# Forget-gate sums of the first attention: from selector matmuls to a DMA broadcast into the bias tile, with three weight tiles ahead of the head loop

## The reference

```python
z = h @ w_in                                   # (256 tokens, all projections)
fq, fk, fv, ff, dq, dk, dv, ga, gb = split(z)  # ff: 8 columns, the forget gates
log_f = log_sigmoid(ff + b_fgate)              # (8 heads, 256)
F = cumsum(log_f, axis=-1)                     # along the tokens
s = einsum('hqd,hkd->hqk', q, k) * scale + F[:, :, None] - F[:, None, :]
p = softmax(where(k_pos <= q_pos, s, -inf))    # 8 "fox" heads of width 64
o_a = einsum('hqk,hkd->hqd', p, v)
# then 4 "diff" heads (two softmaxes each), gates, output projections,
# a mixture of 32 experts, and a second block with attention and convolution
```

## Time and profile before

| what | value |
| --- | --- |
| median of three runs | 1005.55 us |
| the profiled execution, own time | 1005.98 us |
| its span | 1004.2 us |
| busy: PE, DVE, ACT, POOL | 909.9 (91%), 362.0 (36%), 321.0 (32%), 116.9 (12%) us |
| DMA over the span | 308.62 MB, mean 307 GB/s |
| shares of the chain that ended last | PE 67%, DMA 20%, DVE 4%, issue 3% |

### The profile page before, as it was taken

One profiled execution on the slowest core, in us unless ns is written; L12 is line 12 of the kernel. 1 busy time (PEld: TensorE's weight loads), 2 busy tenths in 40 slices (PEclk: granted clock), 3 DMA queues, 4 the chain that ended last, 5 costly groups with the idle time before them and its releaser, 6 DMA issues.

```text
span 1004.2 us, 26158 instructions
## 1 busy us (share of the span) xinstructions
PE 909.9 (91%) x12047; PEld 788.9 (79%) x12047; DVE 362.0 (36%) x740; ACT 321.0 (32%) x554; POOL 116.9 (12%) x78
## 2 busy tenths in 40 slices
PE   7999999999989898987878777779999999999997
PEld 7887789977767676765656556569989999999995
DVE  4356356843111111111111111125334344873475
ACT  5546646631000000000000000125346555554443
POOL 2110021000000000000000000003311112341122
PEclk9999999999999998999899988899999999999998
DMA  8995296899999999999999999999554444455101
GB/s 283 382 348 187 95 347 231 344 426 404 403 426 424 425 424 425 424 424 426 425 425 426 426 426 424 424 357 369 200 213 168 164 175 169 169 184 202 57 1 43
DMA packets 70861, 308.62 MB, mean 307 GB/s; under 512 B 5152, under 2 KB 11728, under 8 KB 58584
## 3 DMA queue, kind: packets, MB, share of 16 engines
q1 hardware_dynamic: 66816, 302.08, 75.7%
q10 hardware_dynamic: 3928, 4.80, 1.4%
HBM read 305.81 MB, written 2.63 MB: 307 GB/s over the span
## 4 chain that ended last, share of the span: by engine, by line
PE 67%; DMA 20%; DVE 4%; issue 3%; ACT 2%; SPq 2%; POOL 1%; another core or an unknown queue 1%; POOLq 0%; DVEq 0%; ACTq 0%
PE bank L789 66%; DMA ring<-in_w 10%; DMA arena<-in_w 10%; SPq L854 2%; DVE arena L1352 1%; DVE wR L1346 1%; DMA ring<-in_w_in 1%; PE bank L1011 1%; DVE arena L1349 1%; POOL wR L2272 1%; DVE arena L1346 0%; ACT wR L1918 0%; DVE hTR L1352 0%; DVE hTR L1346 0%
## 5 line engine op out<-in xcount | busy, mean ns | idle before, releaser
L789 PE MATMUL bank<-hTR,wR 128*128 128x256 f32 x2520 | 314.3, 285 | 4.3 <-DVE hTR L1352 1.6
L789 PE MATMUL bank<-arena 128*32 128x128 f32 (+7 forms) x4378 | 277.9, 324 | 43.2 <-DMA arena<-in_w 27.3
L789 PEld LDWEIGHTS bank<-hTR,wR 128*128 128x128 f32 x2520 | 305.4, 192 | 8.3 <-issue 4.2
L789 PEld LDWEIGHTS bank<-arena 128*32 128x32 f32 (+5 forms) x4378 | 211.2, 142 | 97.7 <-issue 66.6
L1346 DVE TENSOR_TENSOR wR<-ring,wR 128x1024 fp32r<-128x1024 f32 x108 | 136.9, 1274 | 118.0 <-ACT wR L1918 117.7
L1918 ACT ACTIVATE wR<-ring 128x1024 fp32r<-128x1024 f32 x137 | 143.3, 1054 | 91.0 <-PE bank L789 88.3
L789 PE MATMUL bank<-ring,arena 128*32 128x128 f32 (+3 forms) x2352 | 103.7, 319 | 30.9 <-DMA ring<-in_w 22.0
L789 PEld LDWEIGHTS bank<-ring,arena 128*32 128x32 f32 (+1 forms) x2352 | 68.9, 114 | 51.0 <-issue 31.5
L2063 ACT ACTIVATE arena<-bank,small 128x256 f32<-128x256 f32 x32 | 15.1, 473 | 272.2 <-PE bank L789 272.2
L2272 POOL TENSOR_TENSOR wR<-ring,wR 128x1024 fp32r<-128x1024 f32 x29 | 70.7, 2437 | 265.9 <-ACT wR L1918 265.9
L1680 DVE COPY arena<-bank 128x256 f32<-128x256 f32 x32 | 13.6, 425 | 193.4 <-PE bank L789 193.4
(11 more groups left out here) (190 smaller groups left out, 669.3 us busy)
## 6 DMA issues: line engine op xcount, KB each, us to landing
arena<-in_w SPq DMA_DIRECT2D x53, 2048.0 KB, 39.6
ring<-in_w SPq DMA_DIRECT2D x42, 2048.0 KB, 40.1
ring<-in_w_in SPq DMA_DIRECT2D x25, 2048.0 KB, 10.3
ring<-in_w_ada SPq DMA_DIRECT2D x5, 2048.0 KB, 11.2
arena<-in_w_in SPq DMA_DIRECT2D x4, 2048.0 KB, 13.1
ring<-in_w_o_attn SPq DMA_DIRECT2D x2, 2048.0 KB, 8.3
ring<-in_w_out SPq DMA_DIRECT2D x2, 2048.0 KB, 7.9
ring<-in_w_in SPq DMA_DIRECT2D x2, 1024.0 KB, 9.0
```

What stands on the lines that cost most here:

```text
L789: return pe.e.matmul(o, l, r, start=start, stop=stop)
```

## The change

The matmuls with the selector go, and so do the selector, its input and its load (one of six loads that `s_consts` counts, so 96 becomes 80). After `cumsum`, ACT writes `negF` to a small DRAM tensor `fbuf` (8 x 256, step `sums_out`). After `rbuf`, ACT waits for that DMA and issues two more (step `sums_in`), which read the rows of `fbuf` and write them on all 128 partitions into `Bf`: first 8 x 128 numbers on each partition, then 8 x 256. The step `bf` is DVE's alone: it waits for all three DMAs (`s_fbuf` at 48) and adds `Fq` and the mask in place. Three fills stand between `sums_in` and `bf` 0 (tiles 17, 18, 19), where one stood behind `bf` 0. The `bf` steps no longer take turns in banks 2 and 3. The eviction of the gate tiles no longer waits for the last `bf`.

```diff
+        fbuf = nc.dram_tensor("fbuf", [8, 256], F32, kind="Internal").ap()
...
         O1.add("cumsum")
+        O1.add("sums_out")
         next(fill)
         O1.add("rbuf")
-        PB.use(("bf", 0), SR.next())
+        O1.add("sums_in")
+        for _ in range(3):
+            next(fill)
         O1.add("bf", 0)
-        next(fill)
...
             if i < 6 and i % 2 == 0:
-                PB.use(("bf", i // 2 + 1), SR.next())
                 O1.add("bf", i // 2 + 1)
...  TensorE
-            elif what == "bf":
-                u = U_["bf", a[0]]
-                may_write(pe, u)
-                pe.wait_ge(s_consts, 96)
-                emptied(pe, U_["cum"])
-                for s in range(2):
-                    last = mm(pe, banks[u.bank][:, 256 * s:256 * s + 256], selc[0:8, 2 * a[0] + s, :], negF[0:8, :], True, True)
-                last.then_inc(u.full, 1)
...  VectorE
                 elif what == "bf":
-                    u = U_["bf", a[0]]
-                    filled(v, u)
-                    emptied(v, U_["cum"])
-                    v.wait_ge(s_consts, 96)
-                    filled(v, U_["hT1", 3])
-                    for s in range(2):
-                        h = 2 * a[0] + s
+                    v.wait_ge(s_consts, 80)
+                    v.wait_ge(s_fbuf, 48)
+                    for h in (2 * a[0], 2 * a[0] + 1):
                         for n, (x, y) in enumerate(SEG):
-                            last = stt(Bf[:, h, x:y], banks[u.bank][:, 256 * s:256 * s + y - x], Fq[:, 8 * n + h:8 * n + h + 1],
-                                       mask[:, x:y], ALU.add, ALU.add)
-                    last.then_inc(u.free, 1)
+                            last = stt(Bf[:, h, x:y], Bf[:, h, x:y], Fq[:, 8 * n + h:8 * n + h + 1], mask[:, x:y], ALU.add, ALU.add)
+                    last.then_inc(s_bf, 1)
...  ScalarE
+                elif what == "sums_out":
+                    emptied(s, U_["cum"])
+                    eng.dma_start(fbuf, negF[0:8, :]).then_inc(s_fbuf, 16)
+                elif what == "sums_in":
+                    s.wait_ge(s_fbuf, 16)
+                    filled(s, U_["hT1", 3])
+                    for x, y in SEG:
+                        src = bass.AP(fbuf.tensor, fbuf.offset, [[0, 128], [256, 8], [1, y - x]])
+                        eng.dma_start(Bf[:, :, x:y], src).then_inc(s_fbuf, 16)
```

More of the change, by code:

```diff
@@ L163, in bass_two_hybrid_blocks @@
         OH, RB, MR, RR = area(71, 384), area(72.5, 8), area(73, 384), area(74.5, 384)
-        selc, biasD = area(64, 8, 128), area(76, 4, 384)
+        biasD = area(76, 4, 384)
         fqT, fkT, fv = area(36, 4, 256), area(40, 4, 256), area(44, 2, 512)
@@ L396, in bass_two_hybrid_blocks @@
                              "mh", "fg"))
+        s_fbuf, s_bf = sem("fbuf"), sem("bf")
         s_accsq, s_xg = sem("accsq"), sem("xg")
@@ L868, in sync_program @@
             eng.dma_start(kpack[:, :], t["k_pack"]).then_inc(s_consts, 16)
-            eng.dma_start(selc[0:8], t["k_sel"]).then_inc(s_consts, 16)
             eng.dma_start(bfg[0:8, :], t["b_fgate"][0].rearrange("(a b) -> a b", b=1)).then_inc(s_consts, 16)
@@ L1029, in first_steps_pe @@
                 may_write(pe, u)
-                pe.wait_ge(s_consts, 96)
+                pe.wait_ge(s_consts, 80)
                 mm(pe, banks[u.bank][0:8, 0:384], RB[0:32, :], OH[0:32, :], True, True).then_inc(u.full, 1)
@@ L1469, in first_steps @@
                     if m < 8:
-                        emptied(v, U_["bf", m // 2])
+                        v.wait_ge(s_bf, m // 2 + 1)
                     else:
@@ L1950, in first_steps @@
                         filled(s, u)
-                        emptied(s, U_["bf", 3])
                         s.wait_ge(s_rrow, 16)
@@ L2379, in constants @@
     tri = np.concatenate([np.zeros((128, 128), f), np.triu(np.ones((128, 128), f)), np.ones((128, 128), f)], 1)
-    sel = np.zeros((8, 8, 128), f)
-    for h in range(8):
-        sel[h, h] = 1.0
     n = 255 - np.arange(384)
@@ L2389, in constants @@
     iota = np.tile(np.arange(SLOTS, dtype=f), (128, 1))
-    return {"k_ident": np.eye(128, dtype=f), "k_diff": diff, "k_sel": sel, "k_bucket": oh, "k_future": future,
+    return {"k_ident": np.eye(128, dtype=f), "k_diff": diff, "k_bucket": oh, "k_future": future,
             "k_pack": np.concatenate([mask, tri, iota], 1)}
```

## The result

The changed kernel takes 1012.63 us (median of 7 runs, 1011.70 to 1017.31) against 1005.82 us for the one before in 7 runs: ratio 1.0072, 95% interval 1.0058 to 1.0086. It is slower by some 7 us; the forecast was 1017.3, with a range of 1009 to 1022. The profiled execution took 1013.8 us at a span of 1011.9, 7.7 more than the span before.

What follows compares the result with a forecast made beforehand. The weight stream sets the pace, but PE's ordered list in the first block releases it. Start +9.6, rest of loop -2.2, loop end +2.7, clock +1.7 sum to +11.8 us: 1017.3 us, range 1009 to 1022.

Steps and rivals of the forecast that it cites:

- Mechanism and sign: Start of head loop: bias DMAs queue behind `rbuf` on 8 engines, PE stands some 12 us; slower, chance 0.85.
- When the bias tile lands: Bias DMAs on ACT's queue behind `rbuf`: tile lands between 83.2 and 88.4 us, taken as 87.5.
- The tail of 1.7 us: Estimated time from the bias DMAs' last packets until the semaphore rises: 1.7 us.
- near the upper end: Choice of 87.5 us for the landing, since the ada2 weight chunk would share the engines no later than `rbuf` ends.
- L: Time at which the bias tile lands: 83.2 to 88.4 us, taken as 87.5.
- The chain from there to `p_turn` 0: DVE and ACT steps from the bias tile's landing to `p_turn` 0: 7.0 us, so `p_turn` 0 at 94.5 us.
- ACT held at its issue: Issues behind `rbuf` may hold ACT 1.5 us or until 78 us, moving PE's idle time earlier at no cost of its own.
- PE's savings: Four `bf` steps leave PE, 4.5 us, and a 0.73 us wait; `bf` 2 and 3 give -2.2 us, or -1.1.
- The end of the loop: Fills run out two tiles early, so PE waits ahead of `p_turn` 11: +2.7 us, from +1 to +4.
- The clock: PE's clock falls to 0.50 for about 3.4 us after the stand: +1.7 us, from 0 to 3.4.
- a shift of PE reaches the end at full size: First block: any delay or saving of PE before 180 us delays the weight stream and counts fully in kernel time.
- The rival of the other sign: Bias DMAs don't queue behind `rbuf`, tile lands at 74.7 us, kernel faster by 2.1 us (1003.4); chance 0.09.

Runs made afterwards that it cites:

- run 1: Changed kernel with the DRAM-to-DRAM copy `rbuf` issued 40 us later, at iteration 7 of the head loop; ratio 0.9999 to the kernel before, median 1006.79 us.
- run 5: Changed kernel with the two bias DMAs issued first and the copy `rbuf` straight behind them on the same queue; ratio 1.0008 to the kernel before, median 1006.93 us.
- run 11: The reordered kernel of run 9 with the copy `rbuf` back ahead of the bias DMAs; ratio 1.0071 to the kernel before, median 1012.80 us.
- run 3: Changed kernel with the copy `rbuf` at its place but its access patterns turned, slowest dimension 128 instead of 8; ratio 1.0048 to the kernel before, median 1011.57 us.
- run 2: Control: the kernel before, with the copy `rbuf` issued at iteration 7; ratio 0.9990 to the kernel before, median 1005.90 us.
- run 10: Control: the kernel before, with `fox_norm` 1 and `diff_mix` 3 moved earlier; ratio 1.0008 to the kernel before, median 1006.70 us.
- run 12: Changed kernel with the copy `rbuf` issued between the two bias DMAs; a single time, 1016.84 us.
- run 7: Changed kernel with `fbuf` rows of 384 numbers, written by two small DMAs, and one bias DMA instead of two; ratio 1.0072 to the kernel before, median 1013.13 us.
- run 9: Run 1's kernel with `sums_in` one fill later, `fox_norm` 1 and `diff_mix` 3 earlier, iteration 13 without its second fill; ratio 0.9973 to before, median 1003.39 us.
- run 4: The kernel before, matmuls for the bias kept, with only the three fills placed ahead of `bf` 0; ratio 1.0057 to the kernel before, median 1013.35 us.

## Why the forecast was right, and where its sizes were off

**Mechanism and sign: right.** The bias DMAs queue behind `rbuf` on 8 busy engines, and the late tile holds the softmax chain. Shown by taking the copy away (run 1), by swapping (run 5), by putting it back (run 11) and, for the 8 engines, by run 3. The controls (runs 2, 10) do nothing.

**When the bias tile lands: the term that was mis-sized.** I chose 87.5 between 83.2 and 88.4; it was 82.6, just below the low bound, so `p_turn` 0 came at 89.21 instead of 94.5 and the shift was +4.4 instead of +9.6. The end of the packets was about right: 81.5 by the sum without ada2, 82.1 in the trace. The tail of 1.7 us was too long: DVE starts 0.5 us behind the last packets. The main error is the choice "near the upper end", 4.3 us for ada2, for which ada2 had to be issued early. I had written that a held ACT would delay ada2 and bring L down, by 2 us at most, and did not apply it: ACT was held, ada2 came at 78.65, 3.1 us later than before, and the packets ended only 0.6 us later than summed without it. Runs 11 and 12, with ada2 at 76.57 and 77.65, have the tile at 85.6 and 86.4: the upper half of the range is real, under another order. Run 7 has 82.67 with ada2 at 74.81, so the issue time of ada2 alone does not set L, and how much of the error is due to it stays argued. The chain from there to `p_turn` 0 took 6.6 us for 7.0.

**ACT held at its issue: right**, both that it happens (till 74 us) and that it moves the idle time without a price of its own (run 7).

**PE's savings: 4.5 us priced right, but partly not collected.** `bf` 2 and 3 were to give 2.2 us. From `p_turn` 0 to `qk` 14 only 0.4 us came out: the shift went from +4.4 to 166.59 - 156.48 - 6.1 = +4.0. `p_turn` 1 waits 1.40 us for ACT now, where the matmuls of `bf` 2 had covered the norm. The low end of that term, 1.1, was still too high.

**The end of the loop: +2.7, measured +2.7.** From `qk` 14 to `p_turn` 11 13.3 us, and 16.7 before, less 6.1. Of this 1.95 us show as waits.

**The clock: +1.7 taken, about +1.1 on the path.** The 3.4 us of low clock that the term rests on come from the windows of 2 us from 230 to 236 before, at 0.74, 0.50 and 0.91. After the change there are two falls. The one in tile 19 (1.5 us) lies inside the time that PE waits for the tile anyway; the one behind `p_turn` 11 is what lengthens the way from there to the product with w_pb: 191.30 - 179.89 = 11.4 us, where it was 183.56 - 173.21 = 10.35.

**Sum.** 4.4 - 0.4 + 2.7 + 1.0 = +7.7 in the profile; the medians differ by 6.8. The forecast's +11.8 loses 5.2 us with L, gains 1.8 with the savings that fell short, and loses 0.7 with the clock: +7.7. So part of the closeness is luck: with L as it was and the savings as summed the change would have cost 1.8 us less. That a shift of PE reaches the end at full size holds for the change (+7.7 at w_pb and in the span) and less well elsewhere: +7.8 and +6.4 in run 11, -3.6 and -2.0 in run 9.

**A cost that the forecast didn't see: the place of the fills.** It took the fills ahead of the loop to be free at the start. Run 4 shows that in the old kernel this move alone costs as much as the whole change. With the DMA in place of the matmuls the same move costs only its end (run 1 equals before). So the two parts of the change depend on each other, and what made it slow is neither of them but the copy that stood ahead in the queue.

**The rival of the other sign** had put the sum without the queue at -2.1 us. Run 1 gave 0.0: its tile landed at 76.3 instead of 74.7, and 1.4 us went at `p_turn` 1. The bias DMAs were issued at 68.09, no later than the 68.5 assumed, but from 68 to 70 us they had only 24% of the engines' time, beside a weight chunk with 79%, and over 68 to 78 us their packets took 38 ns each (49.2% of 16 engines for 2080 packets), not 35. The gain is there only once the order is mended (run 9).

## What to carry to other kernels

Before you put a small, urgent DMA on a queue, look at what stands ahead of it there and on how many engines that lies; swapping the two issues won here what the change had lost. When work leaves the engine that sets the pace, ask what it was covering: the freed 4.5 us turned into waits until DVE's and ACT's steps were put in a new order. A filler moved from one end of a loop to the other is paid at both ends, at the far one by a missing cover and at the near one by what it now stands between.

## What the runs showed of the hardware that I had not expected

- The copy's own issue is never held: 0.75 to 0.78 us wherever it lies on 8 engines. The issues behind it are: 2.24 and 3.88 us in the changed kernel, 3.64 in run 12, 0.41 and 3.35 with the copy on 16 engines (run 3); 1.03 us for both without it ahead (runs 1 and 5). The rule is open.
- 8 KB written to DRAM beside a weight chunk landed after 4.33 us, more than the 3.5 us of a 64 KB load.
- PE's clock fell to 0.50 in run 4 after waits of only 1.07 and 0.52 us with narrow matmuls between them; a wide tile behind took 5.12 us, not 3.1. In run 1 it stayed at 1.00 through waits of 0.81 and 1.40 us.
- Two versions of the bias fetch issued at the same moment landed 3 us apart (82.6 and 85.6) when a chunk of the other queue came 2.1 us earlier; one with rows of 1536 bytes kept 82.7 with the chunk 3.8 us earlier (run 7).
